# A hybrid SSD and attention layer on one core: GpSimd's steps of the scan re-ordered, decay loads ahead of the x loads, copies of P ahead of exponentials

## The chip, the cores and the metric

The kernel is one program on one core of a Trainium2 chip. The metric is the device time in microseconds of one execution. Engines are named as the profile names them: PE is the matrix engine, DVE the vector engine, ACT the scalar engine, POOL is GpSimd, SP issues DMAs. All times below are microseconds unless marked ns.

## The reference

One decoder layer over 512 tokens of width 1024, all in float32. The part that matters here:

```python
h = rmsnorm(x, norm_mix_w); proj = h @ w_in            # columns: z, xbc, dt, q, k, v, f
xbc = silu(causal_dwconv(xbc)); dt = softplus(dt + dt_bias)
# scan, chunks of 128 tokens, 16 heads of 64, 2 groups of 128 states:
CB     = einsum('bclgn,bcsgn->bcgls', Cc, Bc)
y_diag = einsum('bcgls,bcgrls,bcsgrp->bclgrp', CB, decay, Xdt)
states = einsum('bclgn,bclgr,bclgrp->bcgrpn', Bc, decay_to_end, Xdt)   # then a scan over the 4 chunks
y_off  = einsum('bclgn,bcgrpn,bclgr->bclgrp', Cc, h_in, exp(cum))
y = y_diag + y_off + X * d_skip
y_ssm = rmsnorm(y * silu(z), ssm_norm_w)
q, k = rmsnorm(q), rmsnorm(k)                           # per head of 64
logits = q.k/sqrt(d) + (c_t - c_s), causal; P = softmax(logits); out = P @ V
y_att = rmsnorm(out, att_out_norm_w)
x = x + concat(y_ssm, y_att) @ w_out
x = x + moe(rmsnorm(x, norm_ffn_w))                     # 32 experts, top group, top 2 in it
```

## The kernel before

**Passes.** All projections are cut into blocks of 512 columns, and a block into four passes of 128 tokens (for xbc of 128 features). A pass is 8 tiles `pass_tile(n, k)`, each of three matmuls (L1406 to L1408), because each float32 operand is split in a high and a low part. ACT makes the high part of each 256 KB weight slot (`high`, L1023), DVE or POOL the low part (`weight_low`, L282). A slot's high part waits until the slot ten back has been used, and SP loads slot i once slot i-6 has its low part. So the highs and lows of a block come in a burst: seven behind the third pass of a block, one behind the fourth.

**The scan's stage** is the loop over i from 0 to 16 in the block of PE at L1575 and on. Pass i is a pass over q (i below 8) or k (i from 8), and i = 16 is the first pass over v. Four passes belong to one chunk c = i // 4 of the scan. Beside the passes PE makes, for every pass, the four transposes of the normalised q or k, `qk_transpose(i)` (L1567), which stand after pass i+1; and for each chunk `cb(c)` (L1535, C times B), `diag(c, w)` for w from 0 to 3 (L1525, the decay matrix times x for four heads, into bank 7; the profile shows eight instructions), `y_off(c, g)` (L1547, the contribution of the state, into bank 4) and `state(c, g)` (L1560). `diag(c, 0)` and `diag(c, 1)` stand inside the third pass of the chunk (i % 4 == 2), `diag(c, 2)`, `diag(c, 3)` and `y_off(c, 1)` behind it, between passes.

DVE's order in iteration i: `qk_sum(i)` (L2069), `qk_scale(i)` (L2075, waits for ACT's two small steps of `qk_rstd`), then by i % 4: 0 and 1: two `m_product` each (L2088); 1: `y_add(c, 0)`; 2: `y_add(c, 1)` (L2097, L2103, L2105); 3: `state_keep(c, 0)` and `(c, 1)` (L2114, L2120, L2122); and last the low parts of that pass. `y_add` reads bank 7 and bank 4, and `diag(c, 2)` waits for `y_add(c, 0)` to have read bank 7.

POOL's order for chunk c: `causal_decays(c+1)` (L779), `gate(c)` (L774, y times silu(z)), `scaled_x(c+1)` (L767, x times the decay to the end, what `state` multiplies), `skip_term(c+1)` (L759, x times d_skip; y is one buffer, so the x of chunk c+1 is loaded into it after `gate(c)`). SP loads that x with `load_conv_chunk` (L578) and the state's decays with `load_decay_out` (L584), between two weight slots.

**Attention** runs under the w_out passes over the scan's half (n from N_SO = 44 to 51). `attention_steps(n, k)` puts 24 steps behind tiles. In PE's step s: `scores(s + 2)` (L1611, waits for the row maxima that free its bank), `pv(s - 1)` (L1639, waits for both copies of P), `p_transpose(s)` (L1622). ACT and DVE take the even and the odd half: ACT the exponentials `p_exp` (L1194), the copy `pt_store` (L1202), and per pair of heads `heads_copy` (L1209), `heads_high` (L1214), `heads_square` (L1219); DVE `row_max` (L2175), its `pt_store` (L2192), `p_scale` (L2184), `heads_low` (L2197). In the passes n = 47 and n = 51 a weight slot's high and low part also stand at each k (`slot_after`).

**The rest.** From the passes over the attention half of w_out (n from 52) on, 100 MB of expert weights are loaded; each load waits for a pass, or for an expert that has been computed.

## Time and profile before

| | us |
|---|---|
| median of 3 runs | 723.89 (723.05 to 724.41) |
| the profiled execution | 723.36 |
| its span, first to last instruction | 721.7 |
| PE busy in the span | 682.1 (95%) |
| DVE, ACT, POOL busy | 387.8, 291.4, 130.8 |
| the scan's stage | about 144 to 266 |
| attention | about 306 to 414 |
| experts | about 488 to 721 |

How to read it: the stages follow one another on PE, and PE is nearly always busy up to the experts; there the DMA engines are (DMA share 1.0 at some 410 GB/s). A PE that reads as busy can still have lost time: matmuls are pipelined, and a wait of a few tenths often shows only as a longer distance between two starts. So starts of the same kind of instruction are compared with each other.

### The profile page before, as it was taken

The numbers are of one execution on the slowest core, as the hardware profiler recorded it, in microseconds if no ns is written. First come the engines' busy times: TensorE is split into PE (matmuls) and PEld (weight loads), VectorE is DVE, ScalarE is ACT, GpSimd is POOL, SyncE is SP. The second block draws the span as 40 slices with busy tenths as digits, with TensorE's granted clock in tenths as the row PEclk, the third lists the DMA queues.
The fourth block names the chain that finished last, engine by engine and source line by source line (L and its number), as shares of the span: only waits on it lengthen the run. The fifth ranks groups of instructions, "written<-read, shape, count | busy, mean of one in ns | idle before, by whom it ended". The sixth has DMA issues, their size and how long they took to land. (4 is left out here: it accounts for less than half of the span.)

```text
span 721.7 us, 10665 instructions
## 1 busy us (share of the span) xinstructions
PE 682.1 (95%) x3860; PEld 472.0 (65%) x3860; DVE 387.8 (54%) x845; ACT 291.4 (40%) x651; POOL 130.8 (18%) x167
## 2 busy tenths in 40 slices
PE   8999999989999999999999999989999977887994
PEld 7878878867777888766766788887434333332552
DVE  6866658878878765777787543461222211121221
ACT  5934424365645545665666423221212111121210
POOL 2300010114222110022222110010123331122321
PEclk9999999999999999999999999969999999998999
DMA  8333255426264343191030079689999999999994
GB/s 297 93 115 117 76 165 160 137 80 173 75 161 135 99 146 101 46 353 56 16 103 1 3 277 424 247 336 364 411 418 416 404 410 399 425 417 414 415 398 136
DMA packets 61447, 162.77 MB, mean 226 GB/s; under 512 B 14216, under 2 KB 25636, under 8 KB 50128
## 3 DMA queue, kind: packets, MB, share of 16 engines
q1 hardware_dynamic: 49408, 144.64, 53.8%
q0 software_dynamic: 6880, 9.02, 4.2%
q10 hardware_dynamic: 5104, 8.39, 3.1%
q8 instruction: 33, 0.54, 0.3%
q14 instruction: 22, 0.18, 0.1%
HBM read 157.67 MB, written 20.28 MB: 247 GB/s over the span
## 5 line engine op out<-in xcount | busy, mean ns | idle before, releaser
L1817 PE MATMUL bank<-s_gu,s_xgT 128*64 128x512 f32 x352 | 85.6, 643 | 17.0 <-DMA s_gu<-in_w_expert_up_dram 17.0
L282 DVE TENSOR_TENSOR s_wl<-s_raw,s_wh 128x512 fp32r<-128x512 f32 x116 | 89.8, 821 | 12.3 <-ACT s_wh L1023 12.1
L1023 ACT ACTIVATE s_wh<-s_raw 128x512 fp32r<-128x512 f32 x120 | 72.6, 628 | 41.9 <-PE bank L1408 17.9
L1406 PE MATMUL bank<-s_wh,s_hTh 128*128 128x512 f32 x192 | 78.7, 410 | 0.0
L1817 PEld LDWEIGHTS bank<-s_gu,s_xgT 128*64 128x64 f32 x352 | 29.0, 147 | 72.6 <-issue 72.6
L1408 PE MATMUL bank<-s_wh,s_hTl 128*128 128x512 f32 x192 | 75.2, 391 | 0.0
L1407 PE MATMUL bank<-s_wl,s_hTh 128*128 128x512 f32 x192 | 74.8, 390 | 0.0
L1322 ACT ACTIVATE s_sg<-bank,s_slot_scale 128x256 f32<-128x256 f32 x16 | 7.6, 474 | 150.0 <-PE bank L1817 115.0
L1848 PE MATMUL bank<-s_dn,s_hidT 128*64 128x512 f32 x256 | 58.5, 598 | 1.6 <-DVE s_hidT L2393 1.6
L2393 DVE COPY s_hidT<-bank 128x256 f32<-128x256 f32 x16 | 6.8, 424 | 95.2 <-PE bank L1826 95.2
L2426 DVE SCALAR_TENSOR_TENSOR s_yrow<-bank,s_slot_scale,s_xg 128x512 f32<-128x512 f32 x30 | 21.1, 747 | 46.9 <-PE bank L1848 43.4
L1406 PEld LDWEIGHTS bank<-s_wh,s_hTh 128*128 128x128 f32 x192 | 36.1, 188 | 10.1 <-issue 2.8
L899 POOL DMA_INDIRECT s_xg<-x_rows,s_slot_rows x16 | 16.6, 1038 | 142.7 <-DVE s_yrow L2426 108.4
L1408 PEld LDWEIGHTS bank<-s_wh,s_hTl 128*128 128x128 f32 x192 | 36.0, 188 | 7.9
L1407 PEld LDWEIGHTS bank<-s_wl,s_hTh 128*128 128x128 f32 x192 | 36.1, 188 | 7.4 <-issue 0.7
L1406 PE MATMUL bank<-s_hTh,s_wh 128*128 128x512 f32 x96 | 39.2, 408 | 0.0
L1408 PE MATMUL bank<-s_hTh,s_wl 128*128 128x512 f32 x96 | 37.7, 392 | 0.0
L1407 PE MATMUL bank<-s_hTl,s_wh 128*128 128x512 f32 x96 | 37.4, 390 | 0.0
L1848 PEld LDWEIGHTS bank<-s_dn,s_hidT 128*64 128x64 f32 x256 | 16.9, 136 | 31.2 <-issue 27.1
L1194 ACT ACTIVATE s_Pe<-s_Pe,s_nmax 128x512 f32<-128x512 f32 (+3 forms) x41 | 22.6, 554 | 25.1 <-DVE s_nmax L2175 25.1
L779 POOL TENSOR_SCALAR_AFFINE_SELECT s_decay_rows<-s_decay_rows 128x2048 f32<-128x2048 f32 x4 | 8.5, 2137 | 108.2 <-DMA s_decay_rows<-decay_rows 108.2
L2047 DVE SCALAR_TENSOR_TENSOR s_acc<-s_up,s_cvec,s_acc 128x512 f32<-128x512 f32 x36 | 27.1, 752 | 1.3
(307 smaller groups left out, 1375.1 us busy)
## 6 DMA issues: line engine op xcount, KB each, us to landing
s_dn<-in_w_expert_down_dram SPq DMA_DIRECT2D x28, 1024.0 KB, 28.8
s_gu<-in_w_expert_gate_dram SPq DMA_DIRECT2D x26, 1024.0 KB
s_gu<-in_w_expert_up_dram SPq DMA_DIRECT2D x24, 1024.0 KB, 29.6
s_raw<-in_w_in_dram SPq DMA_DIRECT2D x88, 256.0 KB, 4.1
s_raw<-in_w_out_dram SPq DMA_DIRECT2D x32, 256.0 KB, 3.6
s_gu<-in_w_expert_up_dram SPq DMA_DIRECT2D x12, 512.0 KB, 28.2
s_decay_rows<-decay_rows SPq DMA_DIRECT2D x4, 1024.0 KB, 4.7
s_gu<-in_w_expert_gate_dram SPq DMA_DIRECT2D x8, 512.0 KB
```

The source lines that it names most:

```text
L282: eng.tensor_tensor(low, full, high.bitcast(F32), ALU.subtract).then_inc(sem(f"{what}_low_{low_engine(what, i)}"), 1)
L779: pool.affine_select(out=m["decay_rows"][:], in_=m["decay_rows"][:], compare_op=ALU.is_ge, fill=MASKED, base=0, pattern=[[0, H], [1, P]], ...
L899: pool.indirect_dma_start(out=token_rows(p), out_offset=None, in_=x2_dram[:, :], in_offset=bass.IndirectOffsetOnAxis(ap=slot_rows[:, p:p + ...
L1023: act.activation(wh[:, i % HL, :], raw[:, i % RAW, :], ACT.Copy).then_inc(sem("w_high"), 1)
L1194: act.activation(p_tile(v), p_tile(v), ACT.Exp, bias=nmax[:, v:v + 1], scale=-1.0, accum_out=rsum[:, v:v + 1]).then_inc(sem("p_exp"), 1)
L1406: pe.matmul(dst, ah, bh, start=start, stop=False)
L1407: pe.matmul(dst, ah, bl, start=False, stop=False)
L1408: return pe.matmul(dst, al, bh, start=False, stop=stop)
L1817: last = pe.matmul(ps[j][r, :].rearrange("p (w f) -> p w f", w=2), m["xgT"][:, j, k, r], gu[:, half, :, k, :], start=(k == 0), stop=(k == ...
L1848: last = pe.matmul(ps[6 + nb][r, :], m["hidT"][:, j, at:at + CAP], dn[:, half, q, nb * BLK:(nb + 1) * BLK], start=(q == 0), stop=(q == 1))
L2047: ins = dve.scalar_tensor_tensor(out=a, in0=up[:, f % 2, t:t + T], scalar=tap[t], in1=a, op0=ALU.mult, op1=ALU.add)
L2426: dve.scalar_tensor_tensor(out=m["yrow"][:, j, cols], in0=ps[6 + nb][:], scalar=gates, in1=token_rows(p)[:, cols], op0=ALU.mult, op1=ALU.a ...
```

## The change

In the scan:

- `diag` is placed inside passes everywhere: (c, 0) and (c, 1) move from tiles 1 and 3 of the chunk's third pass to tiles 2 and 4; (c, 2) and (c, 3) from behind that pass to tiles 1 and 3 of the fourth, and `y_off(c, 1)` to tile 4 of the fourth. `cb(0)` moves two tiles later.
- POOL's `scaled_x(c)` waits for all four `m_product` of its chunk; `gate(c)` waits for both `state_keep` of its chunk (the last one for the last `qk_sum`); `skip_term` comes ahead of `scaled_x`.
- SP loads the state's decays ahead of the x of a chunk, and no longer waits for that chunk's `y_add`; the x load moves to just before the block's last slot.
- For chunk 0 the copy of y onto itself (L2107) goes; the exponentials of dte and etot and the product that uses them stand behind the first decays and `m_product`s, and `qk_square(0)` ahead of the load of ACT's table.

In attention: ACT does `heads_copy` and `pt_store` ahead of the exponentials, and DVE the low part of the slot of (n, k) behind the step of (n, k).

```diff
--- before.py
+++ after.py
@@ -579,13 +579,16 @@
 
             def load_decay_out(c):
 
-                sp.wait_ge(sem("y_whole"), 2 * c)
+                if c == 1:
+                    sp.wait_ge(sem("y_diag"), 2)
+                else:
+                    sp.wait_ge(sem("y_whole"), 2 * (c - 1))
                 for odd in range(2):
                     sp.dma_start(decay_out[odd * HD:(odd + 1) * HD, :, :], decay_dram[c].rearrange("(q s) t -> s q t", s=2)[odd].partition_broadcast(HD))\
                         .then_inc(sem("decay_out_in"), 16)
 
             def load_first_bias():
-                sp.wait_ge(sem("y_whole"), 2 * TC)
+                sp.wait_ge(sem("y_whole"), 2 * (TC - 1))
                 for odd, name in ((0, "first_bias_even"), (1, "first_bias_odd")):
                     sp.dma_start(m[name][:], bias_dram[odd].partition_broadcast(P)).then_inc(sem("bias_in"), 16)
 
@@ -622,8 +625,9 @@
                 elif i == 6 * KC:
                     load_conv_chunk(0)
                 elif i in (7 * KC + KC // 2, 8 * KC + KC // 2, 9 * KC + KC // 2):
+                    load_decay_out(i // KC - 6)
+                elif i in (8 * KC - 1, 9 * KC - 1, 10 * KC - 1):
                     load_conv_chunk(i // KC - 6)
-                    load_decay_out(i // KC - 6)
                 load_weight_slot(sp, i)
 
             sp.wait_ge(sem("yT_low"), KC)
@@ -762,6 +766,7 @@
             def scaled_x(c):
 
                 if c < TC - 1:
+                    pool.wait_ge(sem("m_done"), 4 * c + 4)
                     if c:
                         pool.wait_ge(sem("state_done"), 2 * c)
                     pool.tensor_tensor(heads(Xs[:]), heads(X[:, c, :]), over(dte[:, c, :], P, H, HD), ALU.mult)\
@@ -769,7 +774,14 @@
 
             def gate(c):
 
-                pool.wait_ge(sem("y_whole"), 2 * c + 2)
+                if c:
+                    pool.wait_ge(sem("y_whole"), 2 * c)
+                else:
+                    pool.wait_ge(sem("y_diag"), 2)
+                if c < TC - 1:
+                    pool.wait_ge(sem("state_kept"), 2 * c + 2)
+                else:
+                    pool.wait_ge(sem("qk_sum"), 16)
                 pool.wait_ge(sem("z_stored"), TC + c + 1)
                 pool.tensor_tensor(zs[:, c, :], y[:], zs[:, c, :], ALU.mult).then_inc(sem("gated"), 1)
 
@@ -811,8 +823,8 @@
             for c in range(TC - 1):
                 causal_decays(c + 1)
                 gate(c)
+                skip_term(c + 1)
                 scaled_x(c + 1)
-                skip_term(c + 1)
             gate(TC - 1)
             causal_bias(0)
 
@@ -1159,13 +1171,12 @@
                     act.wait_ge(sem("y_folded"), c)
                 act.activation(Pe[:, 0:2, :].rearrange("p a t -> p (a t)"), zs[:, c, :], ACT.Square).then_inc(sem("y_squared"), 1)
 
+            qk_square(0)
             act.preload_act_table_set("natural_log_exp_and_others")
-            act.wait_ge(sem("steps_known"), 4)
-            act.activation(dte[:], dte[:], ACT.Exp).then_inc(sem("dt_acts"), 1)
-            act.activation(etot[:], tot[:, :, 0:H], ACT.Exp).then_inc(sem("dt_acts"), 1)
             for i in range(16):
                 n = N_QK + i
-                qk_square(i)
+                if i:
+                    qk_square(i)
                 qk_rstd(i)
                 if i:
                     qk_store(i - 1)
@@ -1176,6 +1187,10 @@
                     decays(i // 4, 1)
                     if i:
                         decay_out_exp(i // 4)
+                    else:
+                        act.wait_ge(sem("steps_known"), 4)
+                        act.activation(dte[:], dte[:], ACT.Exp).then_inc(sem("dt_acts"), 1)
+                        act.activation(etot[:], tot[:, :, 0:H], ACT.Exp).then_inc(sem("dt_acts"), 1)
                 if i % 4 == 1:
                     decays(i // 4, 2)
                     decays(i // 4, 3)
@@ -1247,12 +1262,11 @@
                         high(i)
                     for s in attention_steps(n, k):
                         ahead = steps_of(s + 2) if s + 2 < NEV else ()
+                        if s and s % NEH == 0:
+                            heads_copy(s // NEH - 1)
+                        pt_store(2 * s)
                         if ahead:
                             p_exp(2 * ahead[0])
-                        pt_store(2 * s)
-                        if s and s % NEH == 0:
-                            heads_copy(s // NEH - 1)
-                        if ahead:
                             p_exp(2 * ahead[0] + 1)
                         if len(ahead) > 1:
                             p_exp(2 * ahead[1])
@@ -1572,21 +1586,20 @@
                     pass_tile(N_QK + i if i < 16 else N_V, k)
                     if i == 0 and k == 1:
                         x_transpose(NTR - 1)
-                    if i == 1 and k == 1:
+                    if i == 1 and k == 3:
                         cb(0)
-                    if i >= 2 and i % 4 == 2 and k in (1, 3):
-                        diag(i // 4, k // 2)
+                    if i >= 2 and i % 4 == 2 and k in (2, 4):
+                        diag(i // 4, k // 2 - 1)
+                    if i >= 2 and i % 4 == 3 and k in (1, 3):
+                        diag(i // 4, 2 + k // 2)
+                    if i > 4 and i % 4 == 3 and k == 4:
+                        y_off(i // 4, 1)
                 if i == 0:
                     continue
                 qk_transpose(i - 1)
                 c, step = (i - 1) // 4, (i - 1) % 4
                 if step == 0 and c:
                     y_off(c, 0)
-                if step == 1:
-                    if c:
-                        y_off(c, 1)
-                    diag(c, 2)
-                    diag(c, 3)
                 if step == 2 and c < TC - 1:
                     state(c, 0)
                     state(c, 1)
@@ -2103,8 +2116,6 @@
                     dve.tensor_tensor(yo, yo, ps[4][:], ALU.mult).then_inc(sem("y_off_scaled"), 1)
                     dve.wait_ge(sem("y_off_scaled"), 2 * (c - 1) + g + 1)
                     dve.tensor_tensor(y[:, cols], y[:, cols], yo, ALU.add).then_inc(sem("y_whole"), 1)
-                else:
-                    dve.tensor_copy(y[:, cols], y[:, cols]).then_inc(sem("y_whole"), 1)
 
             def state_keep(c, g):
 
@@ -2125,14 +2136,14 @@
             for i in range(16):
                 qk_sum(i)
                 qk_scale(i)
-                if i == 0:
-                    dve.wait_ge(sem("dt_acts"), 5)
-                    dve.tensor_tensor(dte[:], dte[:], sp[:, :, 0:H], ALU.mult).then_inc(sem("scales_known"), 1)
-                    dve.wait_ge(sem("scales_known"), 1)
                 c = i // 4
                 if i % 4 == 0:
                     m_product(c, 0)
                     m_product(c, 1)
+                    if c == 0:
+                        dve.wait_ge(sem("dt_acts"), 5)
+                        dve.tensor_tensor(dte[:], dte[:], sp[:, :, 0:H], ALU.mult).then_inc(sem("scales_known"), 1)
+                        dve.wait_ge(sem("scales_known"), 1)
                 if i % 4 == 1:
                     m_product(c, 2)
                     m_product(c, 3)
@@ -2219,9 +2230,6 @@
 
             for n in range(N_SO, N_AO):
                 for k in range(KC):
-                    for i in slot_after(n, k):
-                        if low_engine("w", i) == "dve":
-                            weight_low(dve, i)
                     for s in attention_steps(n, k):
                         ahead = steps_of(s + 2) if s + 2 < NEV else ()
                         if ahead:
@@ -2235,6 +2243,9 @@
                             p_scale(s + 1)
                         if s and s % NEH == 0:
                             heads_low(s // NEH - 1)
+                    for i in slot_after(n, k):
+                        if low_engine("w", i) == "dve":
+                            weight_low(dve, i)
                     if n == N_AO - 1 and k == 0:
                         heads_low(NHP - 1)
                 if n == N_SO:
```

## Rows read from the trace of the kernel before

**Rows 1.** PE's waits, 140 to 270: who waited for what, us, times, longest.

```profile
PE bank L1535 <- ACT s_BC L1089: 0.9, 1, 0.9
PE bank L1525 <- DVE s_y L2097: 0.8, 1, 0.8
...
PE bank L1567 <- DVE s_qn L2075: 0.5, 1, 0.5
```

**Rows 2.** PE's timeline, transposes of q and k: start, us, instruction, count.

```profile
149.88 0.60 PE L1567 MATMUL bank<-s_ident,s_qn 128*128 128x128 f32 x4
...
158.10 0.60 PE L1567 MATMUL bank<-s_ident,s_qn 128*128 128x128 f32 x4
...
166.07 0.60 PE L1567 MATMUL bank<-s_ident,s_qn 128*128 128x128 f32 x4
...
174.31 0.66 PE L1567 MATMUL bank<-s_ident,s_qn 128*128 128x128 f32 x4 [0.47 <-DVE s_qn L2075]
...
180.95 0.60 PE L1567 MATMUL bank<-s_ident,s_qn 128*128 128x128 f32 x4
...
189.41 0.60 PE L1567 MATMUL bank<-s_ident,s_qn 128*128 128x128 f32 x4
...
197.45 0.60 PE L1567 MATMUL bank<-s_ident,s_qn 128*128 128x128 f32 x4
...
205.06 0.60 PE L1567 MATMUL bank<-s_ident,s_qn 128*128 128x128 f32 x4
...
211.69 0.60 PE L1567 MATMUL bank<-s_ident,s_qn 128*128 128x128 f32 x4
...
220.15 0.60 PE L1567 MATMUL bank<-s_ident,s_qn 128*128 128x128 f32 x4
...
228.79 0.60 PE L1567 MATMUL bank<-s_ident,s_qn 128*128 128x128 f32 x4
...
236.43 0.60 PE L1567 MATMUL bank<-s_ident,s_qn 128*128 128x128 f32 x4
...
242.81 0.60 PE L1567 MATMUL bank<-s_ident,s_qn 128*128 128x128 f32 x4
...
259.29 0.60 PE L1567 MATMUL bank<-s_ident,s_qn 128*128 128x128 f32 x4
...
265.22 0.60 PE L1567 MATMUL bank<-s_ident,s_qn 128*128 128x128 f32 x4
```

**Rows 3.** POOL's timeline in the scan's second chunk.

```profile
194.35 2.78 POOL L774 TENSOR_TENSOR s_zs<-s_y,s_zs 128x1024 f32<-128x1024 f32 x1 [1.22 <-DVE s_y L2105]
199.84 2.00 POOL L767 TENSOR_TENSOR s_Xs<-s_X,s_dte 128x1024 f32<-128x1024 f32 x1 [2.72 <-PE bank L1560]
```

**Rows 4.** DVE's timeline over the same stretch.

```profile
194.18 8.21 DVE L282 TENSOR_TENSOR s_wl<-s_raw,s_wh 128x512 fp32r<-128x512 f32 x7
202.32 0.67 DVE L2069 TENSOR_REDUCE s_qss<-s_sq 128x8 f32<-128x512 f32 x1
203.60 0.69 DVE L2075 TENSOR_TENSOR s_qn<-bank,s_qr 128x512 f32<-128x512 f32 x1 [0.61 <-ACT s_qr L1016]
```

**Rows 5.** The instructions of L578, which load a chunk's x into y.

```profile
DMA to landing us min/median/max: 4.1/6.7/8.0
```

**Rows 6.** PE's timeline in attention, scores of every third step.

```profile
349.85 1.13 PE L1611 MATMUL bank<-s_kT,s_qT 64*128 64x512 f32 x4
...
362.75 1.39 PE L1611 MATMUL bank<-s_kT,s_qT 64*128 64x512 f32 x4
...
378.40 1.13 PE L1611 MATMUL bank<-s_kT,s_qT 64*128 64x512 f32 x4
```

**Rows 7.** DVE's groups, 355 to 373: busy, mean ns, idle before.

```profile
L282 DVE TENSOR_TENSOR s_wl<-s_raw,s_wh 128x512 fp32r<-128x512 f32 x8 | 6.4, 847 | 1.1 <-ACT s_wh L1023 1.1
```

**Rows 8.** The chain that ended last, 361 to 376: start, us, what.

```profile
368.63 0.47 ACT s_PT L1202
```

**Rows 9.** Stages by window: us, busy of PE, PEld, DVE, ACT, POOL, clock, DMA share, GB/s.

```profile
567.00:624.00 57.00, 46.87 (x212) 18.68 (x210) 11.01 (x19) 10.26 (x24) 13.33 (x12) 0.93 1.02 409
```

## The prediction

> **What bounds the kernel now.** I read the page first: PE is busy for 95% of the span, and the slices say that this holds up to the experts. From there it is the loads of the experts' weights: between 567 and 624 the DMA engines' share is 1.02 [rows 9], and the chain of work that ended last is SP's queue there. But these loads are released by passes and experts in their order, from n = 52 on, so what PE gains ahead of n = 52 moves the whole rest. I take it one for one. The question is thus how much PE stands still in the scan and in attention.
>
> PE's list of waits names only a part: 0.9 at `cb(0)` for ACT's last silu, 0.8 at `diag(0, 2)` for `y_add(0, 0)`, 0.5 at the transposes [rows 1]. So I compared intervals between transposes of successive passes [rows 2]:
>
> - with nothing beside the pass (the last pair of rows): 265.22 - 259.29 = 5.93
> - with `y_off(1, 0)` and two `diag` inside the pass: 189.41 - 180.95 = 8.46, so 2.53 for them
> - with `y_off(1, 1)` and two `diag` between passes: 197.45 - 189.41 = 8.04, so 2.11
> - with two `state`: 205.06 - 197.45 = 7.61, so 1.68
> - with `cb`: 242.81 - 236.43 = 6.38, so 0.45.
>
> I take these as free of waits, since no row of wait falls in them. `y_off` is eight transposes' worth, 0.9 by the four transposes that make up 0.45 of a plain interval; then two `diag` cost 1.62 inside a pass and 1.21 between passes. Every interval over its like is a wait:
>
> - 149.88 to 158.10 is 8.22, against 5.93 + 1.62 = 7.55: 0.67
> - 158.10 to 166.07 is 7.97, against 5.93 + 1.21 = 7.14: 0.83
> - 166.07 to 174.31 is 8.24, against 7.61: 0.63
> - 174.31 to 180.95 and 205.06 to 211.69 are 6.64 and 6.63, against 6.38: 0.26 + 0.25
> - 220.15 to 228.79 is 8.64, against 8.04: 0.60.
>
> With `cb(0)`'s 0.9 the scan loses 4.1.
>
> **The scan, part by part.** *Why DVE is late.* Seven lows in a row took 8.21 [rows 4] where seven at the 0.68 of L2069's size take 4.8: 3.4 too long. In that stretch POOL runs `gate` for 2.78 and `scaled_x` for 2.00 [rows 3]. The change moves both away from the burst: `gate(c)` behind `state_keep`, `scaled_x(c)` to `m_done`.
>
> A rule speaks to this. The Trainium skill, "SBUF — State Buffer", section "SBUF: two separate sides", says that VectorE and GpSimd share a port pair under an exclusive lock, which a VectorE instruction with two SBUF inputs and a GpSimd one that reads SBUF cannot hold together. The trace agrees for the burst (3.4 over). By the rule it also speaks against the change: `scaled_x(c)` now starts just when `y_add(c, 0)` runs, whose last instruction reads y and decay_out from SBUF, and would be held for about 2.0 - 1.4 = 0.6 in chunks 1 and 2; no row shows this pair.
>
> *Each wait.* `cb(0)` two tiles later: 2 x 0.7 of pass ahead of it, more than the 0.9, so it goes. In 149.88 to 158.10 `m_product(0, 0)` waits behind dte's product and `scaled_x(0)`; both move behind, `qk_square(0)` no longer waits for the table load, and `diag` stands one tile (0.7) later: 0.67 goes. `diag(0, 2)` had to wait for `y_add(0, 0)`; it now stands a pair of tiles behind it, 1.4 more than the 0.83: goes. The same for `y_off(2, 1)` (0.60). 0.63 + 0.26 + 0.25 are the late `qk_scale` and `state_keep` behind the burst. Their new dates: `diag(c, 3)` and `y_off(c, 1)` at tiles 3 and 4 end at 4.4 and 6.1 from the fourth pass's start; two steps of `y_add` make 7.5; seven lows 4.8; `qk_sum`, rstd, `qk_scale` 0.67 + 0.61 + 0.69 = 2.0 [rows 4]: 14.3. The transposes that need it stand at 8.1 + 7.6 = 15.7 in chunks 1 and 2 (spare 1.4), as much later than `y_add` in chunk 0, where no `y_off` stands (spare about 3), and at 8.1 + 5.9 = 14.0 in chunk 3, where no `state` follows: a new wait of 0.3. All in all 4.1 is won, 0.3 lost.
>
> *What it costs.* A tile of a pass is (5.93 - 0.45) / 8 = 0.7. Four pairs of `diag` go from 1.21 to 1.62: 4 x 0.41 = 1.6. Three `y_off(c, 1)` inside a pass: bounded by nothing and by the 0.4 that the split of a whole pair costs; I take 0.05 each, for they are full-width like transposes: 0.15. `qk_square(0)`, decays and exps are the same instructions in another order: nothing, ACT has them under PE's pass 2. The removed copy of y: DVE's, under PE: nothing by itself.
>
> *What is queued behind new waits.* POOL's `gate(c)` waits for `state_keep`, and `skip_term(c+1)` and `scaled_x(c+1)` behind it. SP's x load waits for `gate(c)`; behind it are the block's last slot, whose low part comes before `gate` ends anyway or just after, and `load_decay_rows`, due a chunk later: nothing. From `state_keep`'s end: gate 2.8, landing 6.7 (4.1 to 8.0) [rows 5], `skip_term` 2.0 like `scaled_x` of its size [rows 3]: 11.5, and 0.7 of `y_add(c+1, 0)`: 12.2. `state_keep` ends at 14.3 + 4 x 0.7 = 17.1, which is 1.4 behind the transposes at 15.7; `diag(c+1, 2)` comes 6.4 + 8.5 + 1.8 behind these, so 15.3 after `state_keep`: spare 3.1 (1.8 at the slowest landing). `load_decay_out` is earlier than before: never late. If `gate` holds DVE's `qk_sum` (no row shows it), that is up to 2.1 later, on a chain that ends 1.4 + 0.7 + 2.0 = 4.1 behind transposes whose successors come at 6.4: spare 2.3, so nothing.
>
> The scan: 4.1 - 0.3 - 1.6 - 0.15 = **2.1** (0.8 to 3.2).
>
> **Attention.** Three steps take 362.75 - 349.85 = 12.9, and the next three, with as many tiles, 378.40 - 362.75 = 15.65 [rows 6]: 2.75 lost, all in n = 47, where eight lows of 847 ns on average, 6.8 in all, lie in DVE's stream [rows 7]. In this stretch DVE sets the pace: lows, then `row_max`, then its `pt_store`, on which `pv` waits; at 368.63 the last is ACT's `pt_store`, behind an exponential that waited for `row_max` [rows 8]. The change puts the low of the step's own tile behind the step. Three steps (s = 12, 13, 14) are led by such a low: each saves 0.6 to 0.7 once, less what the next step inherits; DVE's amount of work stays, but lows fall into its idle time (1.1 in front of lows alone). ACT's copy alone gives little, since DVE's copy ends within 0.4 of it; both together give some 1.1 by step 14 and 1.75 by step 15. I take **1.75** (0.4, if DVE's copy stays late, to 2.75). Elsewhere attention loses about nothing that the change touches: ACT's exponentials for step s + 2 come up to 0.5 later, and `p_scale` needs them a whole step (4) later.
>
> **The sum.** 723.36 - 2.1 - 1.75 = 719.5 for the profiled execution; the median stands 0.53 above that one, so I forecast 723.89 - 3.85 = **720.0**, between 718.6 and 721.6 if all goes this way.
>
> **Rivals.**
>
> 1. *DVE is late again.* POOL still meets DVE: `gate` the low and `qk_sum`, `skip_term` the `m_product`s, `scaled_x` the end of `y_add`. For it: rows 3 and 4 show 3.4 lost to two POOL instructions, and the work of POOL is the same. Against: 1.4 to 3.1 spare. If 3.4 per chunk come back in chunks 1 and 2, each loses 2.0, the scan gains -1.9 and attention 1.75: 724.0. If only half comes, 0.3 each, nothing visible. Attention not mended and half of the scan: 1.2 gained, 722.7.
> 2. *It doesn't reach the end.* The loads at 409 GB/s set the end [rows 9], and if some of them don't start earlier the gain is swallowed: 723.9, no change. Against: every load waits for PE.
> 3. *Slower: the late x.* `gate(c)` to landing to `skip_term` to `y_add(c+1, 0)` to `diag(c+1, 2)`. It decides from a landing of 6.7 + 3.1 = 9.8 on; at 12.0, three chunks lose 2.2 each: 723.89 - 3.85 + 6.6 = 726.6. For it: the load was up to 8.0, and other loads queue. Against: the decays, that shared the engines with it, now go ahead.
> 4. *The whole of both wins*, with cheaper splits: 723.89 - 5.9 = 718.0.
>
> **How the numbers follow.** Forecast 0.62; rival 1 in its mild form (722.7) 0.14, in its full form (724.0) 0.04; rival 2 0.07; rival 3 0.05; rival 4 0.08. The range 718.0 to 722.9 holds the forecast, rival 4 and the mild rival 1. A measurement tells 0.2% (1.4) from no change: faster is below 722.4, which the forecast and rival 4 give, and a third of the mild rival 1: 0.77. Slower is above 725.3: rival 3 and a little: 0.06. The rest, 0.17, is within 0.2%.
>
> **What would show it.** Intervals between the transposes: 7.6, 7.6, 7.6, 6.4 in chunk 0, and 8.5, 8.5, 7.6, 6.4 in the others, 6.2 at the end. Right would be: PE's waits of rows 1 gone; lows in bursts of 4.8; `diag` pairs at 1.6; attention's three steps at 362.75 about 13.9. Wrong: a wait of `diag` for y (rival 3), of transposes for qn (rival 1), splits dearer than 0.41, or a span whose first 414 shrink by more than its end.

## The result

The changed kernel takes 715.76 (715.27 to 716.63, five runs) against 723.89 (722.35 to 724.41, five runs): the ratio is 0.9900, with a 95% interval of 0.9886 to 0.9914. That is 8.1 less; the forecast was 3.85 less, and its range ended at 718.0. The sign was right, the size was not: by these medians the gain is more than twice the forecast.

The same pair was measured twice more among the experiments and gave 0.9921 (0.9908 to 0.9933) and 0.9929 (0.9913 to 0.9946). Counted by the ratio at 723, the three gains are 7.2, 5.7 and 5.1; counted between medians they are 8.1, 6.2 and 5.8. So part of the first gain is spread between comparisons, and what is left of it needs a cause in the code.

The profiled execution of the changed kernel took 715.27, with a span of 713.7. PE's timeline shows the transposes of q and k in the first chunk, the second and the last (start, us, instruction, count):

```profile
147.41 0.60 PE L1581 MATMUL bank<-s_ident,s_qn 128*128 128x128 f32 x4
154.96 0.60 PE L1581 MATMUL bank<-s_ident,s_qn 128*128 128x128 f32 x4
162.49 0.60 PE L1581 MATMUL bank<-s_ident,s_qn 128*128 128x128 f32 x4
...
184.91 0.60 PE L1581 MATMUL bank<-s_ident,s_qn 128*128 128x128 f32 x4
193.37 0.60 PE L1581 MATMUL bank<-s_ident,s_qn 128*128 128x128 f32 x4
201.02 0.60 PE L1581 MATMUL bank<-s_ident,s_qn 128*128 128x128 f32 x4
...
255.24 0.60 PE L1581 MATMUL bank<-s_ident,s_qn 128*128 128x128 f32 x4
261.56 0.66 PE L1581 MATMUL bank<-s_ident,s_qn 128*128 128x128 f32 x4 [0.25 <-DVE s_qn L2088]
```

The intervals are 7.55, 7.53, then 8.46 and 7.65, and 6.32 at the end. The forecast for them was 7.6, 7.6, 8.5, 7.6 and 6.2. From the first of these transposes to the last it is 114.15, against 115.34 in [rows 2]. PE's waits from 140 to 425 are down to two. Those of [rows 1] are gone, and the second one here is the wait of 0.3 that was forecast for the last transposes:

```profile
PE bank L1635 <- DVE s_Pe L2195: 0.5, 1, 0.5
PE bank L1581 <- DVE s_qn L2088: 0.2, 1, 0.2
```

Attention, as in [rows 6], every third step's scores:

```profile
346.24 1.13 PE L1624 MATMUL bank<-s_kT,s_qT 64*128 64x512 f32 x4
...
359.13 1.13 PE L1624 MATMUL bank<-s_kT,s_qT 64*128 64x512 f32 x4
...
372.00 1.13 PE L1624 MATMUL bank<-s_kT,s_qT 64*128 64x512 f32 x4
```

The steps of n = 47 take 12.87 in place of 15.65, no longer than the three before them. The whole 2.8 came back, where I had taken 1.75.

A third difference stands where nothing was edited. The first transposes come at 147.41 in place of 149.88, 2.47 earlier. 0.3 of this is there already at 90, and some 0.9 is `cb(0)`'s wait. Most of the rest begins near 104, where ACT in the kernel before waited longer for a store of x. The two answers below are ACT's waits from 92 to 108, first of the kernel before, then of the changed one:

```profile
ACT s_xs L1089 <- DMA conv_rows<-s_xs: 3.2, 2, 2.8
```

```profile
ACT s_xs L1101 <- DMA conv_rows<-s_xs: 1.1, 1, 1.1
```

So four things were open: whether this belongs to the change, which part of the scan's edits gains, why attention gave more, and whether the end follows PE one for one.

### The profile page after: what moved, and what is told of

It reads as the page before. It is cut to its first block, busy times and chain, and to the rows that moved or that the text cites. A ratio compares the mean times of both kernels' runs of the same rounds, so it can differ in the third digit from the quotient of the medians.

```text
span 713.7 us, 10669 instructions
## 1 busy us (share of the span) xinstructions
PE 677.1 (95%) x3860; PEld 468.1 (66%) x3860; DVE 374.3 (52%) x843; ACT 288.9 (40%) x651; POOL 132.0 (18%) x167
## 4 chain that ended last, share of the span: by engine, by line
PE 75%; DMA 10%; SPq 9%; DVE 2%; issue 1%; ACT 1%; POOL 0%; POOLq 0%; DVEq 0%; ACTq 0%
PE bank L1420 16%; PE bank L1422 15%; PE bank L1421 15%; PE bank L1830 6%; SPq L427 5%; DMA s_gu<-in_w_expert_gate_dram 4%; DMA s_gu<-in_w_expert_up_dram 4%; PE bank L1624 3%; PE bank L1635 3%; PE bank L1652 3%; PE bank L1861 3%; SPq L461 2%; PE bank L1801 2%; SPq L479 2%; PE bank L1539 1%
## 5 line engine op out<-in xcount | busy, mean ns | idle before, releaser
L1830 PE MATMUL bank<-s_gu,s_xgT 128*64 128x512 f32 x352 | 83.9, 632 | 16.8 <-DMA s_gu<-in_w_expert_up_dram 16.8
L1035 ACT ACTIVATE s_wh<-s_raw 128x512 fp32r<-128x512 f32 x120 | 70.8, 625 | 50.9 <-DMA s_raw<-in_w_in_dram 24.5
L282 DVE TENSOR_TENSOR s_wl<-s_raw,s_wh 128x512 fp32r<-128x512 f32 x116 | 77.7, 715 | 12.7 <-ACT s_wh L1035 12.5
L1420 PE MATMUL bank<-s_wh,s_syTh 128*128 128x512 f32 x64 | 27.4, 428 | 0.0
L1420 PE MATMUL bank<-s_wh,s_xTh 128*128 128x512 f32 x64 | 25.7, 402 | 0.5 <-DVE s_xTl L1949 0.5
```

The source lines that it names most:

```text
L282: eng.tensor_tensor(low, full, high.bitcast(F32), ALU.subtract).then_inc(sem(f"{what}_low_{low_engine(what, i)}"), 1)
L1035: act.activation(wh[:, i % HL, :], raw[:, i % RAW, :], ACT.Copy).then_inc(sem("w_high"), 1)
L1420: pe.matmul(dst, ah, bh, start=start, stop=False)
L1830: last = pe.matmul(ps[j][r, :].rearrange("p (w f) -> p w f", w=2), m["xgT"][:, j, k, r], gu[:, half, :, k, :], start=(k == 0), stop=(k == ...
```

## The experiments

Three stretches of PE's timeline are compared in all traces. The **head** runs from the last transposes of z ahead of the scan (near 90) to the first of q. The **stage** runs from there to the last transposes of k. The **three steps** are those of n = 47. The bounds were read from each kernel's timeline; "sum" is their difference to the kernel before, taken as 58.28 (the head in its second trace), 115.5 (the mean of the five traces whose scan is unedited) and 15.66. "Measured" is the ratio with its interval, and the gain in us at 723.

| kernel | head | stage | three steps | sum | measured |
|---|---|---|---|---|---|
| before, first trace | 59.40 | 115.34 | 15.65 | | |
| before, second trace | 58.29 | 115.79 | 15.69 | 0.3 | 0.9999 (0.9982 to 1.0015) |
| changed, first | 57.19 | 114.15 | 12.87 | -5.2 | 0.9900 (0.9886 to 0.9914), -7.2 |
| changed, second | 57.19 | 114.18 | 12.86 | -5.2 | 0.9921 (0.9908 to 0.9933), -5.7 |
| changed, third | 57.19 | 113.99 | 12.86 | -5.4 | 0.9929 (0.9913 to 0.9946), -5.1 |
| scan alone | 58.17 | 114.05 | 15.66 | -1.6 | 0.9952 (0.9937 to 0.9967), -3.5 |
| attention alone | 58.20 | 115.31 | 12.86 | -3.1 | 0.9956 (0.9942 to 0.9970), -3.2 |
| ACT's order alone | 58.36 | 115.61 | 14.04 | -1.4 | 0.9970 (0.9958 to 0.9983), -2.2 |
| low parts alone | 58.27 | 115.61 | 14.08 | -1.5 | 0.9954 (0.9939 to 0.9970), -3.3 |
| POOL's old order | 57.19 | 121.24 | 12.87 | 1.9 | 1.0024 (1.0012 to 1.0036), +1.7 |
| splits undone | 57.19 | 113.46 | 12.86 | -5.9 | 0.9919 (0.9903 to 0.9934), -5.9 |
| POOL and loads alone | 58.19 | 112.52 | 15.64 | -3.1 | 0.9956 (0.9944 to 0.9969), -3.2 |
| mixed places | 57.19 | 112.43 | 12.86 | -7.0 | 0.9884 (0.9868 to 0.9900), -8.4 |
| x first | 57.19 | 120.02 | 12.87 | 0.6 | 1.0011 (0.9996 to 1.0026), +0.8 |

(The 0.9900 is 7.2 at 723; the two medians differ by 8.1.)

**The scan's edits alone.** The changed kernel with ACT and DVE of attention as before.

> All edits of the scan (POOL's order, decays ahead of x, diag and y_off at other tiles, DVE's and ACT's first iteration), attention as before. Theory A (each part passes to the end one for one, and what is over comes from a stretch that nobody changed): from the first transposes (149.88 in before) to those before the v pass's end (265.22) the profile shows some 1.2 us less and ahead of that 1.3 to 2.5 less; the time is 2.3 to 2.5 below before, 721.5, plus whatever TensorE's low clock between 476 and 489 gives back (up to 1.6). Theory B (the 2.5 us ahead of the first transposes belong to the change): the profile again shows the first transposes at 147.4 and the time is 719.5 to 720.2. Theory C (they are the luck of one profiled execution): the first transposes stand at 148.5 to 149 and the store of conv_rows again holds ACT near 100.

Measured 720.09 against 723.0. Its head, 58.17, holds a wait of 0.8 of the transposes of z, the same as the first trace of before has:

```profile
PE bank L1475 <- ACT s_zs L1112: 0.8, 1, 0.8
```

It occurs in these two traces out of fourteen, under an unedited and an edited scan. Without it the head is like the changed kernel's 57.2, so the scan's gain is about 1.0 in the head and 1.5 in the stage. The 1.2 more of the first trace of before are of one execution: theory C. The first transposes stood earlier than C had put them (147.98), since the scan's edits gain in the head too. The time, though, fell where B had put it (719.5 to 720.2): by the ratio it is 3.5 less, 1.0 more than these 2.5, and the trace doesn't say where that is.

**Attention's edits alone, and their two halves.**

```diff
-                        if ahead:
-                            p_exp(2 * ahead[0])
-                        pt_store(2 * s)
                         if s and s % NEH == 0:
                             heads_copy(s // NEH - 1)
+                        pt_store(2 * s)
                         if ahead:
+                            p_exp(2 * ahead[0])
                             p_exp(2 * ahead[0] + 1)
```

is ACT's half; DVE's half moves `weight_low` behind the steps. Both:

> The edits of attention alone (ACT's copy of P and heads_copy ahead of the exponentials, DVE's low parts behind the step), the scan as before. The three steps of n = 47 take 12.9 as in the changed kernel, so 2.8 less. Theory A: 723.9 - 2.8 = 721.1. The rival with the clock (a shift of the router against the low clock gives back up to 1.6 by itself): 719.5 to 720. If the gain is not one for one at the end: over 722. Together with the scan's part it should make the 8.1 of the whole: if both sums are below, the parts depend on one another.

Measured 719.78, 3.2 less, and 12.86 for the three steps. With the scan's 3.5 that makes 6.7, inside the 5.1 to 7.2 of the whole. ACT's half:

> Of attention ACT's order alone: copy of P and heads_copy ahead of the exponentials; DVE's low parts stay in front of the step. The prediction's reading (DVE sets the pace, its copy ends within 0.4 of ACT's): three steps at 15.2 of 15.65, a gain of 0.4, 723.5. The rival (ACT's copy behind an exponential that waits for row_max is the real chain): three steps near 13, a gain of 2.8, 721.1.

DVE's half:

> Of attention DVE's order alone: low parts behind the step; ACT's copy of P stays behind its exponential. The prediction's reading: most of the gain, three steps at 14 to 14.3, 722.3. The rival that ACT's chain is the one that counts: DVE's lows behind the step let row_max come earlier and so ACT's exponential, thus also a gain, but not all: 14.5. If this alone gives all, three steps at 12.9, 721.1.

The three steps take 14.04 with ACT's half and 14.08 with DVE's: each gives 1.6, both 2.8. The expectation of ACT's half fell: it isn't worth 0.4 but 1.6. That of DVE's half came true in its number (14 to 14.3), but not in its meaning, since ACT's half alone gives as much. Two limits show. The first is in ACT's timeline, first of the kernel with DVE's half alone, then of the one with ACT's:

```profile
365.38 0.72 ACT L1194 ACTIVATE s_Pe<-s_Pe,s_nmax 128x512 f32<-128x512 f32 x1 [1.59 <-DVE s_nmax L2175]
...
366.11 0.47 ACT L1202 ACTIVATE s_PT<-bank 128x384 f32<-128x384 f32 x1
```

```profile
364.20 0.49 ACT L1202 ACTIVATE s_PT<-bank 128x384 f32<-128x384 f32 x1 [0.24 <-PE bank L1621]
365.55 0.72 ACT L1194 ACTIVATE s_Pe<-s_Pe,s_nmax 128x512 f32<-128x512 f32 x1 [0.86 <-DVE s_nmax L2174]
```

In the old order the copy of P stands behind an exponential that waits for DVE's `row_max`, and `row_max` stands behind the low parts. Counted from the scores of their step (361.35 and 361.54) the copy starts at 4.8 with the old order and at 2.7 with the new. That alone can't be the gain of this step, for `pv` also waits for DVE's copy, and this one starts 4.5 behind the scores in both halves (365.88 and 366.05); in the kernel before it starts 5.65 behind (368.40 after 362.75), in the changed one 4.4. The second limit is what DVE stands on ahead of that copy. The rows are `heads_low` of the kernel before, of DVE's half, of ACT's half and of the changed one:

```profile
365.31 0.75 DVE L2197 SCALAR_TENSOR_TENSOR s_ayTl<-s_ay,s_cvec,s_ayTh 128x512 fp32r<-128x512 f32 x1 [1.28 <-ACT s_ayTh L1214]
```

```profile
362.79 0.75 DVE L2197 SCALAR_TENSOR_TENSOR s_ayTl<-s_ay,s_cvec,s_ayTh 128x512 fp32r<-128x512 f32 x1 [0.70 <-ACT s_ayTh L1214]
```

```profile
362.95 0.75 DVE L2196 SCALAR_TENSOR_TENSOR s_ayTl<-s_ay,s_cvec,s_ayTh 128x512 fp32r<-128x512 f32 x1 [0.49 <-ACT s_ayTh L1214]
```

```profile
360.41 0.75 DVE L2208 SCALAR_TENSOR_TENSOR s_ayTl<-s_ay,s_cvec,s_ayTh 128x512 fp32r<-128x512 f32 x1 [0.54 <-ACT s_ayTh L1229]
```

`heads_low` waits for ACT's `heads_high`, and behind it stand two low parts, `row_max` and the copy. In the old order `heads_high` and `heads_copy` too stand behind exponentials that wait for `row_max`. So the two engines wait for each other in turn, and either half cuts into it: ACT's half lets `heads_copy` and `heads_high` go earlier, DVE's half lets `row_max`. That each of them saves the same 1.1 in this step, and that only both together bring the last of the three steps from 5.8 to 4.8, is read from these rows; no run separates it further.

**The kernel before and the changed one again.**

> The kernel before once more, unedited: no difference in time. In question are two stretches of its trace: ACT's wait for the store of conv_rows with the transposes of z (1.3 us near 104), and the low clock in the router, 13.7 us long in before's trace and 10.2 in after's, 6.8 in three of the partial kernels. If both are luck, the first transposes stand at 148.2 to 148.5 this time; if they belong to the kernel before, at 149.9 again.

> The changed kernel once more, unedited, for a second trace and a second comparison. Theory A (4.9 us in the changed code, 2.1 + 2.8, and the rest from stretches where nothing was changed and from the low clock in the router): the code's 4.9 stands again in the trace (119 intervals of the scan and the three steps of n = 47), and the time is 5 to 8 below before. If the whole is again 8.1 below before, the 3.2 over the 4.9 are no luck of one execution and need a cause of their own.

The kernel before, again: 722.74 against 722.85, and the first transposes at 148.48, without the wait near 104. The changed one: 716.62 against 722.85. A third comparison of the changed kernel was made later:

> The changed kernel unedited, a third time. The two comparisons so far gave 0.9900 (0.9886 to 0.9914) and 0.9921 (0.9908 to 0.9933), the trace's stretches in which the code differs make 5.5 (2.7 in the scan with cb(0), 2.8 in attention). If this is all: 0.9910 to 0.9930. If there is a gain of 2 us more than the trace's stretches: 0.9885 to 0.9900.

716.09 against 721.86, ratio 0.9929, inside the first range: nothing speaks for more than the trace's stretches here.

**POOL's old order under the rest of the change.**

```diff
-                    pool.wait_ge(sem("m_done"), 4 * c + 4)
...
-                if c < TC - 1:
-                    pool.wait_ge(sem("state_kept"), 2 * c + 2)
-                else:
-                    pool.wait_ge(sem("qk_sum"), 16)
...
+                scaled_x(c + 1)
                 skip_term(c + 1)
-                scaled_x(c + 1)
```

> The changed kernel with POOL's old order in the scan: gate as soon as y is whole, then scaled_x, then skip_term, without the waits for m_product and state_keep. The prediction: the burst of seven low parts goes from 4.8 back to 8.2 and DVE is 3.4 later behind it; the waits of 0.63 + 0.26 + 0.25 return, and with the new places of diag up to 2 us in each of chunks 1 and 2: 1.1 to 4 us slower than the changed kernel. The rival: DVE's spare time behind the new places of diag covers it: within 0.5.

Measured 724.8: 8.2 slower than the changed kernel, and slower than the kernel before by 0.24%. POOL's and DVE's timelines, in the scan's second chunk:

```profile
194.67 2.73 POOL L781 TENSOR_TENSOR s_zs<-s_y,s_zs 128x1024 f32<-128x1024 f32 x1 [2.91 <-DVE s_y L2113]
197.40 2.31 POOL L771 TENSOR_TENSOR s_Xs<-s_X,s_dte 128x1024 f32<-128x1024 f32 x1
...
212.47 1.90 POOL L763 TENSOR_TENSOR s_y<-s_y,s_dskip_of 128x1024 f32<-128x1024 f32 x1 [12.77 <-DMA s_y<-conv_rows]
```

```profile
194.50 6.95 DVE L282 TENSOR_TENSOR s_wl<-s_raw,s_wh 128x512 fp32r<-128x512 f32 x5
...
212.07 2.45 DVE L2096 SCALAR_TENSOR_TENSOR s_M<-s_dec,s_sp,s_cbs 128x128 f32<-128x128 f32 x2
```

The first five low parts take 6.95, where six take 3.69 in the changed kernel (below), and stretch over both of POOL's instructions. Two `m_product`s, 0.35 each when undisturbed, take 2.45 together beside `skip_term`. The transposes that hang on DVE wait 1.30:

```profile
204.62 0.66 PE L1576 MATMUL bank<-s_ident,s_qn 128*128 128x128 f32 x4 [1.30 <-DVE s_qn L2083]
```

In the changed kernel the same stretch reads:

```profile
184.17 1.91 POOL L772 TENSOR_TENSOR s_Xs<-s_X,s_dte 128x1024 f32<-128x1024 f32 x1 [5.69 <-DVE s_M L2101]
...
202.54 2.85 POOL L786 TENSOR_TENSOR s_zs<-s_y,s_zs 128x1024 f32<-128x1024 f32 x1 [14.05 <-issue]
```

```profile
184.72 0.69 DVE L2116 TENSOR_TENSOR s_decay_out<-s_decay_out,bank 128x512 f32<-128x512 f32 x1
185.44 1.18 DVE L2118 TENSOR_TENSOR s_y<-s_y,s_decay_out 128x512 f32<-128x512 f32 x1
...
192.88 3.69 DVE L282 TENSOR_TENSOR s_wl<-s_raw,s_wh 128x512 fp32r<-128x512 f32 x6
197.04 0.69 DVE L282 TENSOR_TENSOR s_wl<-s_raw,s_wh 128x512 fp32r<-128x512 f32 x1 [0.47 <-ACT s_wh L1035]
...
203.04 0.68 DVE L2082 TENSOR_REDUCE s_qss<-s_sq 128x8 f32<-128x512 f32 x1
```

The seven low parts take 4.85 from 192.88 to 197.73. `gate` of 2.85 now meets `qk_sum`, a reduction with one input, which isn't held (0.68). The instruction of `y_add` that reads a bank, at 184.72, runs beside `scaled_x` and isn't held either (0.69). `scaled_x` ends at 186.08, and the last instruction of `y_add`, begun at 185.44, takes 1.18 in place of 0.69: held for 0.5, where `scaled_x` still ran for 0.64. The Trainium skill, "SBUF — State Buffer", section "SBUF: two separate sides", says of this pair that the one which starts first has the ports for its whole instruction; the trace agrees.

**The splits undone.** `diag(c, 2)`, `diag(c, 3)` and `y_off(c, 1)` between the passes again, the rest as changed.

> The changed kernel with diag(c, 2), diag(c, 3) and y_off(c, 1) back between the passes, behind the transposes of the chunk's second pass. The prediction: the pair costs 1.21 in place of 1.62 (1.6 us won in all), but diag(c, 2) waits again for y_add(c, 0), 0.8 in chunk 0 and up to 0.7 more since diag(c, 0) now stands a tile later: 3 to 4 us of wait in four chunks, so 1.5 to 2.5 us slower than the changed kernel. The rival: the splits cost more than the waits that they remove, and this kernel is equal or faster.

716.6, the same as the changed kernel, and its stage is 0.6 shorter (113.46). The rival holds: the waits that the splits were to remove are hardly there, since DVE is no longer late. The intervals with the pair between passes are 8.25 to 8.27, 0.2 over the 8.04 of before, and one wait shows, in chunk 0:

```profile
156.01 1.09 PE L1539 MATMUL bank<-s_M,s_X 128*64 128x128 f32 x16 [0.64 <-DVE s_y L2111]
```

**POOL's order and the loads alone,** on the kernel before.

```diff
+                    pool.wait_ge(sem("m_done"), 4 * c + 4)
...
+                if c < TC - 1:
+                    pool.wait_ge(sem("state_kept"), 2 * c + 2)
+                else:
+                    pool.wait_ge(sem("qk_sum"), 16)
...
-                    load_conv_chunk(i // KC - 6)
                     load_decay_out(i // KC - 6)
+                elif i in (8 * KC - 1, 9 * KC - 1, 10 * KC - 1):
+                    load_conv_chunk(i // KC - 6)
```

and `skip_term(c + 1)` ahead of `scaled_x(c + 1)`.

> On the kernel before, only POOL's new order and waits and the new places of the two loads; PE, DVE and ACT, and attention, as before. If POOL's two-input instructions in front of DVE's are the cause of the late DVE: bursts of seven low parts at 4.8, the 0.63 + 0.26 + 0.25 + 0.60 of wait gone and the diag pairs still at 1.21: 1.7 less, 721.1. The 0.9 of cb(0), the 0.67 and the 0.83 of chunk 0 stay. The rival, that PE's new places are what gains (POOL's order only makes them safe): 722.5 or more.

718.96 against 721.86: 3.2 less by the ratio, where 1.7 was expected. Its stage is 112.52, and thus 1.6 shorter than the changed kernel's. The rows are these:

```profile
148.43 0.60 PE L1573 MATMUL bank<-s_ident,s_qn 128*128 128x128 f32 x4
155.97 0.60 PE L1573 MATMUL bank<-s_ident,s_qn 128*128 128x128 f32 x4
163.60 0.60 PE L1573 MATMUL bank<-s_ident,s_qn 128*128 128x128 f32 x4
...
186.03 0.60 PE L1573 MATMUL bank<-s_ident,s_qn 128*128 128x128 f32 x4
194.07 0.60 PE L1573 MATMUL bank<-s_ident,s_qn 128*128 128x128 f32 x4
```

Interval by interval: 7.54 where [rows 2] have 8.22, so the 0.67 of chunk 0 goes with POOL's order and the loads alone. Its eight `m_product`s take 2.25 there and 3.29 in the kernel before, where `scaled_x(0)` ran beside them. 7.63 where [rows 2] have 7.97 and 7.14 is free of waits, so 0.5 is left of 0.83. And 8.04 where the changed kernel has 8.46. The loads alone on the kernel before weren't run.

**Mixed places.** From this: the changed kernel, with `diag` and `y_off` of chunks 1 to 3 back at the tiles of before, and chunk 0 as changed.

> The changed kernel with diag and y_off of chunks 1 to 3 at the places of before (two diag in tiles 1 and 3, two and y_off(c, 1) between passes) and only chunk 0 at the new ones. From the kernel with the splits undone (intervals of 8.27 there, 8.04 in the kernel before): 3 x 0.4 less than the changed kernel and 0.4 less at the last pair, 1.6 less in all: 115.0 us of scan become 112.6 from the first to the last transposes, and the time is 1 to 1.6 below the changed kernel. If DVE's y_add comes late for the early places, the intervals stay at 8.3 and it is 0.7.

714.2 against 721.86, ratio 0.9884 (0.9868 to 0.9900), and 716.09 for the changed kernel on the same chip. The stage is 112.43, 1.6 below the changed kernel's, as expected; the medians differ by 1.9. It is the fastest of all kernels here, though its interval and the changed kernel's second and third only just part, and the first overlaps it.

**x first.** The changed kernel, with the loads at their old places in SP's queue, x ahead of the decays.

```diff
-                    load_decay_out(i // KC - 6)
-                elif i in (8 * KC - 1, 9 * KC - 1, 10 * KC - 1):
                     load_conv_chunk(i // KC - 6)
+                    load_decay_out(i // KC - 6)
```

> The changed kernel with the x load back in the middle of the block of slots and ahead of the decays' load. The prediction called the order of the loads worth nothing and only never late. The rival: SP now waits for gate, which comes some 8 us later than before, and the weight slots behind it on SP's queue are late: a wait of passes for s_raw or s_wh in each of three blocks, 1 to 5 us slower than the changed kernel. If nothing hangs on it: within 0.5.

722.83 against 721.86, 6.7 slower than the changed kernel. The rival was right that it costs, but by another way. The answers are SP's timeline, ACT's wait from 200 to 262, and PE's timeline:

```profile
205.35 0.38 SPq L578 DMA_DIRECT2D s_y<-conv_rows  x1
205.77 1.27 SPq L587 DMA_DIRECT2D s_decay_out<-decay_rows  x2
```

```profile
ACT s_decay_out L1159 <- DMA s_decay_out<-decay_rows: 10.3, 2, 5.5
```

```profile
219.70 0.66 PE L1538 MATMUL bank<-s_M,s_X 128*64 128x128 f32 x8 [1.87 <-DVE s_y L2109]
```

The decays' load, behind an x load that waits for the late `gate`, starts at 205.77, where it starts at 195.77 in the changed kernel. ACT's exponential of it waits up to 5.5, and ACT's squares and decays stand behind that in order. DVE gets its inputs late, and `diag` waits for y.

Not all of the 6.0 that the stage grew by is wait. In the profiled execution TensorE's granted clock fell in the scan as well, near 254; the other thirteen traces have no fall ahead of the router. The windows (us busy of PE, PEld, DVE, ACT and POOL, clock, DMA share, GB/s):

```profile
251.00:253.00 2.00, 0.30 (x2) 0.00 (x0) 1.97 (x7) 0.78 (x3) 0.00 (x0) 1.00 0.00 0
254.00:256.00 2.00, 2.00 (x5) 1.63 (x6) 1.39 (x3) 0.82 (x3) 0.00 (x0) 0.50 0.00 0
```

PE had been busy for 0.30 of two microseconds, at the second `diag` that waited for y (1.91), and then ran at the lower of its two levels (0.50, 1.2 GHz). The eight instructions of a `diag` that take 0.66 elsewhere took 0.93 there. The interval with this in it is 12.02, where the one with the first such wait (1.87) is 10.40: up to 1.6 is the clock's. Whether the other executions had it too isn't known.

## Why the prediction was wrong

**What failed, in the sum.** The term that was mis-sized is attention's 1.75, which measured 2.8. The scan's 2.1 measured 2.4 to 2.6. Together the stretches where the code differs make 5.2 to 5.4 for a forecast of 3.85. By themselves they would have given 718.5 to 718.7, inside the range. What carried the first comparison below 718.0 is further time that no edit explains, under "What stays open".

**Right: what the scan loses.** I had 4.1 of waits, 0.9 of it at `cb(0)` and 3.2 in the stage. The unedited stage takes 115.5 on the mean of five traces, and 112.4 to 112.5 in the two kernels with POOL's new order and PE's old places in chunks 1 to 3: 3.0 to 3.1 less. These still hold 0.5 of wait or 0.4 of a split pair in chunk 0, so the waits were about 3.5. The head gives 1.0 to 1.1 (58.2 to 58.3 against 57.19). Together about 4.5.

**Right: the price of the split and the new wait.** 4 x 0.41 + 0.15 + 0.3 was 2.1. The intervals with a split pair are 8.46 against 8.04, 0.42 with `y_off` in it. The last one shows 0.25 and 0.28 of wait in two traces and none in the third, where its interval, 6.16, is 0.2 over 5.93. The changed stage is 1.5 to 1.7 above the stage of POOL's order and the loads alone. So the scan came to 1.1 + 1.3 or 1.5 = 2.4 to 2.6 for a forecast of 2.1.

**Wrong: what removes the waits.** I shared them out among the new places of `diag`, `cb` and `y_off` and POOL's order. The runs show that POOL's order with the loads removes 3.0 of the stage's about 3.5 by itself. PE's new places, which cost 1.6, remove the 0.5 that is left in chunk 0, where the split takes 0.4 back, and, with ACT's and DVE's first iteration, give 1.0 in the head; these two weren't run apart. Without POOL's new order they are worth less than nothing: 121.24. The waits of 0.67 and 0.60 and 0.3 of the 0.83 at `diag(0, 2)`, which I had put down to the order on PE, ACT and DVE, were DVE's lateness beside POOL.

**Wrong in size: attention.** The step that failed is "ACT's copy alone gives little, since DVE's copy ends within 0.4 of it". I compared two ends in a trace in which each was late for the other: DVE's copy behind `heads_low`, which waited 1.28 for ACT, and ACT's behind an exponential that waited 1.59 for DVE. ACT's order alone gave 1.6, DVE's alone 1.6, both 2.8. The term 1.75 should have been 2.8, the upper end that I had kept.

**Not in the sum: 1.2 of the trace of before.** The store near 104 was late in two of fourteen traces. It is in no edit, and I had no second trace to see it by; it stretched the profiled execution, and whether it stood in the other executions isn't known.

**The tail, one for one: right, in that nothing is swallowed.** From the first transposes behind attention (447.68 in the kernel before, 441.27 in the changed) to the end of the span it is 274.0 and 272.4, and in all fourteen traces 271.9 to 275.0, while their start varies from 439.3 to 448.7. If the loads kept the end where it was, the tail would grow as the start comes earlier. It is if anything shorter: 272.4 to 274.1 in the five traces that start before 442, and 274.0 to 275.0 in the four that start after 446. Rival 2 fell.

**The rivals.** Rival 1 (DVE late again) is what POOL's old order gives under the new places, dearer than I had it: 7.1 in the trace for a forecast of up to 4. Its chance for this kernel was rightly small, since each of POOL's steps was moved to where DVE's inputs are few. I gave the hold at `y_add` 0.6, and the row has 0.5. Rival 3 (late x) didn't come: the x load lands in 4.0 to 4.7 in the changed kernel's three traces, less than the 6.7 of [rows 5]. I called the earlier decays' load merely "never late", while it is what makes a late `gate` affordable: 6.7. Rival 4 (the whole of both wins, 718.0) had the right order of gain, through attention, not through cheaper splits. The chances had a slip: forecast, rival 4 and a third of the mild rival 1 make 0.75, not 0.77.

**What stays open.** The code's stretches make 5.2 to 5.4. By the ratio, two comparisons of three agree with this (5.7 and 5.1), and the first, 7.2, is 1.9 above the mean of these stretches; between its medians, 8.1, it is 2.7 to 2.9 above. In the first pair of traces the spans differ by 8.0, of which 6.4 lie ahead of 441.27: the code's 5.2 and the 1.2 near 104, which is of a single execution. The other 1.6 are a shorter tail, where nothing was edited. In the three traces of the changed kernel the tail is 272.4, 272.6 and 273.4, in the two of the kernel before 274.0 and 274.5. Kernels that start it in between have 271.9 to 274.7, so whether an earlier start shortens the tail, or it is spread, isn't shown. The kernels with the scan alone and with the low parts alone also measured more than their traces have (3.5 for 2.5, and 3.3 for 1.5).

## What to carry to other kernels

When DVE is late, look first at which POOL instructions with SBUF inputs run in front of DVE instructions with two SBUF inputs, and move POOL to where DVE reads a bank or does a reduction (a plain copy within SBUF is no such place, see below); only then move PE's work, since the waits that would call for it may be gone. An instruction in order that waits for another engine shouldn't stand in front of one whose input is ready and on which the chain hangs; and two copies that end together aren't two limits but may be one cause. Do the cheapest part alone on the chip: here it gave the stage more than the whole did.

## What the hardware showed

The hold between POOL and DVE in this kernel spans a whole instruction. A low part that comes while `gate` runs doesn't get on until `gate` has ended: the second of the burst, taken by itself, stands from 195.11 to 197.94, and `gate` ended at 197.40. One input isn't enough to be free of it. The copy of y onto itself, which the change removes, reads and writes SBUF. In the first trace of before it met `causal_decays` of POOL (161.96 to 163.96), in the second it came ahead of it:

```profile
162.31 1.93 DVE L2107 COPY s_y<-s_y 128x512 f32<-128x512 f32 x1
```

```profile
160.94 0.43 DVE L2107 COPY s_y<-s_y 128x512 f32<-128x512 f32 x1
```

DVE's group of low parts over the scan, of the kernel with POOL's old order and then of the changed one:

```profile
L282 DVE TENSOR_TENSOR s_wl<-s_raw,s_wh 128x512 fp32r<-128x512 f32 x32 | 32.6, 1076 | 0.4 <-ACT s_wh L1030 0.3
```

```profile
L282 DVE TENSOR_TENSOR s_wl<-s_raw,s_wh 128x512 fp32r<-128x512 f32 x32 | 21.6, 726 | 2.3 <-ACT s_wh L1035 2.2
```

TensorE's granted clock fell to the lower of its levels (0.50, 1.2 GHz) in the router (the stage that picks the experts) in every trace, from about 472 to 482 in the changed kernel and from about 476 to 489 in the one before. Ahead of the fall PE had stood still for about half of two microseconds among the ranks (busy for 1.09 of 472 to 474 in the kernel before, and for 1.09 of 466 to 468 in the changed one, where it was busy for 0.99 of 472 to 474, already at the lower level). The windows (us busy of PE, PEld, DVE, ACT and POOL, clock, DMA share, GB/s), first of before, then of the changed kernel:

```profile
476.00:484.00 8.00, 7.27 (x55) 6.89 (x56) 4.97 (x25) 1.40 (x6) 1.01 (x3) 0.50 0.99 408
484.00:500.00 16.00, 15.32 (x112) 12.00 (x113) 4.57 (x18) 3.25 (x10) 3.15 (x3) 0.83 0.78 289
```

```profile
476.00:484.00 8.00, 7.36 (x43) 6.55 (x43) 4.13 (x18) 2.66 (x7) 3.16 (x3) 0.62 0.67 209
484.00:500.00 16.00, 16.00 (x192) 11.96 (x190) 2.55 (x13) 1.62 (x5) 0.77 (x1) 1.00 1.02 409
```

The stretch lasted 13.7 in the first trace of before and 6.8 in its second, and 10.2, 13.6 and 6.8 in those of the changed kernel, so its length isn't the kernel's. The first expert starts up to 1.3 earlier or later for it. The end doesn't follow: in the changed kernel's three traces that expert starts at 482.7, 483.2 and 481.9, and the spans are 713.7, 713.5 and 714.3. The DMA share is 1.02 in the experts [rows 9], so the weights' loads most likely set the end there; no run shows it alone.
